# A block inverse on 128 partitions at once: 64x64 quadrant products replaced by 128x128 ones

## The chip, the core and the metric

The kernel runs on one core of a Trainium2 chip. A core has five engines that run side by side and meet only at semaphores: TensorE (PE, matrix products; its weight loads are shown as PEld), VectorE (DVE), ScalarE (ACT), GpSimd (POOL) and SyncE (SP, which here only starts DMAs). Each works through its own instructions in the order in which they were written. The metric is the device time of one launch in microseconds (us). The kernel before was timed three times: 1513.75, 1516.5 and 1520.16 us.

## The reference

Two transformer blocks in float32 on 256 tokens of width 1024. The first has differential and stick-breaking attention, cross attention and an MLP; the second has a latent attention (MLA), an RWKV-7 recurrence and a mixture of 16384 experts. The change touches the recurrence alone. The reference computes it token by token, per head, with a 64x64 state:

```
def rwkv7_step(state, inp):
    r_t, w_t, k_t, v_t, kk_t, a_t = inp
    sk = jnp.einsum('bhij,bhj->bhi', state, kk_t)
    state = (state * w_t[:, :, None, :]
             - sk[..., None] * (kk_t * a_t)[:, :, None, :]
             + v_t[..., None] * k_t[:, :, None, :])
    y = jnp.einsum('bhij,bhj->bhi', state, r_t)
    return state, y
```

The kernel takes 64 tokens at a time instead (a chunk; 4 chunks x 8 heads). Inside a chunk every token's update depends on those before it through a strictly triangular 64x64 matrix A, and the solution needs the inverse of I + A for each of the 32 pairs of chunk and head.

## The kernel before

All tensors lie with tokens or channels on the 128 partitions. Two chunks are stacked: partitions 0 to 63 hold the even chunk of a pair, 64 to 127 the odd one. So 32 inverses are 16 "problems" (`prob`), each with two chunks in it. Three tiles matter:

- `GB` (tile `hx`): per problem a 128x256 matrix; its first 128 columns are A transposed for both chunks, with zeros where the two chunks would mix (it was masked with `m2`).
- `Xc` and `Yc` (both in tile `pm`): per problem 64 columns, the inverse so far and its transpose, one chunk on each half of the partitions.
- `QX` (tile `pR`): an intermediate product, masked.

The inverse is built in levels. Level 0 is elementwise (`Yc` = I - masked A transposed; `Xc` = `Yc` transposed in 32x32 blocks on DVE). Each level l from 1 to 5 joins blocks of 2^l rows to blocks of twice that: a first product A·`Xc`, a mask (`lx{l}`, from the constants in tile `dst`), a second product with the inverse so far, a subtraction, and for l < 5 a transpose in 32x32 blocks. The 16 problems go in two groups of eight, j = 0 and 1, so that one group is on PE while the other is on DVE.

On PE, `quads` (L1049) makes one product for one group: 16 matrix products of 64x64 by 64x64, the even chunk's in the upper left quarter of the array, the odd chunk's in the lower right, each chunk into a PSUM bank of its own. The profile counts a float32 product as two records, so a call is 32 records of `64*64 64x64`. On DVE, each result is taken chunk by chunk, two operations of 64 partitions x 512 elements (L2283 for the mask, L2291 for the subtraction, both recorded at the helper's line L156), then one transpose (L177) that reads `Xc` and writes `Yc`. The first product of the next level waits for the subtraction; only its second product needs the transpose.

Other work is threaded between the levels, on every engine by the same written plan: the string list `PLAN` says, at each `turns.go()`, which parts take a step: "m" (MLA: squares, rotary embedding, `q2T` transposes, scores `m0` and `m1`, softmax), "t" (transposes of a, b, k, v to token order, `tok`), "k" (the products `GK`, masked into tile `prep`). Four `turns.go()` per level, on PE after each group's product, on DVE before each group's wait. So the order is fixed by hand, and whatever is late holds up what is written behind it.

PSUM has 8 banks. `bank` takes the one that was given back longest ago and waits until its reader is done; `give` names the reader.

`keep(n)` (L142) issues n products of the identity with itself into a bank that is free: 2n records `ps<-cst 128x128`, work without a use other than keeping PE from pausing. The table `KEEP` (L1057) puts 55 of them ahead of ten of the twenty `quads` calls, before the wait for that call's operand.

After level 5, ACT copies the even chunks of `Yc` to tile `rwY` (L1640) and DVE the odd ones (L2298); PE goes on with `values` (`vtok,prep`), which needs all of `GK`, and then with `solved_values` (`pR,rwY`).

Of the kernel before, what the change touches and what calls it, by code (L numbers as in the profile page):

```python
# [13 lines left out]
ALU = mybir.AluOpType  # L14
# [200 lines left out]
def bc(ap, axis, n):  # L215
    u = ap.unsqueeze(axis)
    shape = list(u.shape)
    shape[axis] = n
    return u.to_broadcast(shape)


def constants():
    p = np.arange(128)[:, None]
    f = np.arange(128)[None, :]
    one = lambda m: m.astype(np.float32)
    add = lambda m: np.where(m, 0.0, NEG).astype(np.float32)
    c = {"ident": one(p == f), "iota": np.broadcast_to(np.arange(128, dtype=np.float32), (128, 128)),
         "iota16": np.broadcast_to(np.arange(16, dtype=np.float32), (128, 16))}
    d = {}
    z = np.zeros((128, 128), np.float32)  # L230
    d["maskA"] = np.concatenate([z, add(f <= p)], 1)
    d["maskM"] = np.concatenate([z, add(f // 64 <= p // 64)], 1)
    d["maskS"] = one(p < f)
    d["negtri"] = -one(p >= f)
    d["negones"] = -np.ones((128, 128), np.float32)
    d["blk"] = one(p // 64 == f // 64)
    d["hsel"] = one(p // 64 == np.arange(2)[None, :])
    same = p // 64 == f // 64
    d["m2"] = np.concatenate([one(same & (p < f)), one(same & (p <= f))], 1)
    d["eye2"] = one(p % 64 == np.arange(64)[None, :])  # L240
    for l in range(6):
        m = 1 << l
        lev = (p // (2 * m) == f // (2 * m)) & (p // m % 2 == 1) & (f // m % 2 == 0)
        d[f"lx{l}"] = one(lev)[:, 0:64] + one(lev)[:, 64:128]
        d[f"ly{l}"] = one(lev.T)[:, 0:64] + one(lev.T)[:, 64:128]
    d["rst"] = np.broadcast_to(one(np.arange(256)[None, :] % 64 != 0), (128, 256))
    f1 = np.float32(500000.0) ** (-np.arange(0, 16, 2, dtype=np.float32) / np.float32(16))
    f2 = np.float32(10000.0) ** (-np.arange(16, dtype=np.float32) / np.float32(16))
    d["invf"] = np.broadcast_to(np.concatenate([f1, f2]).astype(np.float32), (128, 24))
    return c, d  # L250
# [10 lines left out]
def build(nc, T, poff, outs, stop=99):  # L261
# [4 lines left out]
    with ctx:  # L266
# [34 lines left out]
        def D(k): return dst[:, doff[k][0]:doff[k][1]]  # L301
# [31 lines left out]
        rt = P0[:, :, :].rearrange("p a b -> p (a b)").rearrange("p (i n d) -> p i n d", i=4, n=16)  # L333
# [82 lines left out]
        pRf = pR[:, :, :].rearrange("p a b -> p (a b)")  # L416
        f2 = lambda t: t[:, :, :].rearrange("p a b -> p (a b)")
        sg, x2_, y_ = hx[:, 0, 0, 0:256], ARt[:, :, 0, :], hx[:, 0, 1, :].rearrange("p (a b) -> p a b", b=256)
        GB = hx[:, :, :, :].rearrange("p i t n -> p (i t n)").rearrange("p (n d) -> p n d", d=256)
# [2 lines left out]
        ysq, TAT, nU = xm("ysq", [128, 16, 64]), xm("TAT", [128, 4, 256]), xm("nU", [128, 2, 512])  # L422
        pmf = pm[:, 0:8, :].rearrange("p a b -> p (a b)")
        c64 = lambda t, k: t[:, 1024 * k:1024 * k + 1024].rearrange("p (n d) -> p n d", d=64)
        QX, Xc, Yc = c64(pRf, 0), c64(pmf, 0), c64(pmf, 1)
        prob = lambda b_, r, i: (b_ * 2 + r) * 4 + i
        halves = [slice(64 * c, 64 * c + 64) for c in range(2)]
        parts = [(tb, lo, hi) for lo, hi in ((0, 384), (384, 640)) for tb in range(2)]
# [93 lines left out]
        def tensor(pe):  # L522
# [87 lines left out]
            for r in range(2):  # L610
                rs = slice(64 * r, 64 * r + 64)
                for hp in range(2):
                    b = pe.bank("z", (r, hp))
# [432 lines left out]

            turns = Turns(mla(), tokens(), products(1))

            def quads(key, lt, rt):  # L1049
                bs = [pe.bank("qd", (*key, c)) for c in range(2)]  # L1050
                for q in range(8):
                    for c, hs in enumerate(halves):
                        last = pe.mm(bs[c][hs, q * 64:q * 64 + 64], lt(c, hs, 8 * key[2] + q), rt(hs, 8 * key[2] + q), True, True)
                last.then_inc("qd_ps", key)


            KEEP = {(1, 0, 0): 3, (1, 1, 0): 4, (1, 1, 1): 5, (2, 0, 0): 15, (2, 0, 1): 9, (2, 1, 0): 3, (4, 1, 1): 3, (5, 0, 0): 5, (5, 1, 0): 5, (5, 1, 1): 3}  # L1057
            for l in range(1, 6):
                for j in range(2):
                    pe.keep(KEEP.get((l, 0, j), 0))  # L1060
                    pe.wait_ge("GB")
                    if l == 1:
                        pe.wait_ge("X0", j)
                    else:
                        pe.wait_ge("XY", (l - 1, j, 1))
                    quads((l, 0, j), lambda c, hs, p: GB[hs, p, 64 * c:64 * c + 64], lambda hs, p: Xc[hs, p, :])
                    turns.go()
                    for c in range(2):
                        pe.give("qd", (l, 0, j, c), "QX", (l, j, c))
                for j in range(2):  # L1070
                    pe.keep(KEEP.get((l, 1, j), 0))
                    pe.wait_ge("QX", (l, j, 1))
                    if l == 1:
                        pe.wait_ge("Y0", j)
                    else:
                        pe.wait_ge("Yt", (l - 1, j))
                    if l < 5:
                        quads((l, 1, j), lambda c, hs, p: Yc[hs, p, :], lambda hs, p: QX[hs, p, :])
                    else:
                        quads((l, 1, j), lambda c, hs, p: QX[hs, p, :], lambda hs, p: Yc[hs, p, :])  # L1080
                    turns.go()
                    for c in range(2):
                        pe.give("qd", (l, 1, j, c), "XY", (l, j, c))
            turns.end("t")
            turns.end("k")
            def values(b_):
# [239 lines left out]
        def scalar(act):  # L1326
# [308 lines left out]
                    turns.go()  # L1635
            turns.end("t")
            for j in range(2):
                act.wait_ge("XY", (5, j, 1))
            act.wait_ge("Y_z")
            act.act(Y[0:64, :, 0:64], Yc[0:64, :, :], ACT.Copy).then_inc("Y_a")  # L1640
            for _ in range(5):
# [107 lines left out]
        def vector(dve):  # L1749
# [522 lines left out]
                    yield  # L2272

            turns = Turns(mla(), tokens(), products(1))
            pv = lambda b, hs: b[hs, :].rearrange("p (a b) -> p a b", a=8)
            for l in range(1, 6):
                for j in range(2):
                    js = slice(8 * j, 8 * j + 8)
                    turns.go()
                    dve.wait_ge("qd_ps", (l, 0, j))  # L2280
                    dve.wait_ge("pm", 11)
                    for c, hs in enumerate(halves):
                        dve.tt(QX[hs, js, :], pv(dve.ps("qd", (l, 0, j, c)), hs), bc(D(f"lx{l}")[hs, :], 1, 8), ALU.mult).then_inc("QX", (l, j, c))  # L2283
                for j in range(2):
                    js = slice(8 * j, 8 * j + 8)
                    turns.go()
                    dve.wait_ge("qd_ps", (l, 1, j))
                    M = Xc if l < 5 else Yc
                    dve.wait_ge("X0" if l == 1 else "Yt", j if l == 1 else (l - 1, j))
                    for c, hs in enumerate(halves):  # L2290
                        v = dve.tt(M[hs, js, :], M[hs, js, :], pv(dve.ps("qd", (l, 1, j, c)), hs), ALU.subtract).then_inc("XY", (l, j, c))  # L2291
                    if l < 5:
                        dve.after(v)
                        dve.tr(Yc[:, js, :].rearrange("p a b -> p (a b)"), Xc[:, js, :].rearrange("p a b -> p (a b)")).then_inc("Yt", (l, j))
            turns.end("k")
            dve.wait_ge("XY")
            dve.wait_ge("Y_z")
# [528 lines left out]
```

## Times and profile before

| | |
|---|---|
| runs | 1513.75, 1516.5, 1520.16 us; median 1516.5 |
| profiled execution | 1519.88 us in all, of it a span of 1517.9 us from the first instruction to the last |
| PE busy | 1468.3 us, 97% of the span |
| DVE, ACT, POOL busy | 1035.8, 725.1, 239.1 us |
| the chain that ended last | PE 84%, DVE 10%, ACT 3% |
| the inverse, levels 1 to 5 with what is threaded between | 555.3 to 617.5 us of the span |

Starts are in us from the span's start. "x32" is the number of records merged into a row. A bracket at the end of a row is idle time of that engine ahead of it, and who ended it. Ends of matrix products are modelled and overlap the next ones, so the distance between the starts of two rows is the better measure of what a PE row takes.

### The profile page before, as it was taken

How to read it: one execution, taken by the hardware profiler on the slowest of the kernel's cores; microseconds unless marked ns; L12 is line 12 of the kernel's file. 1: busy time of each engine (PE TensorE's matmuls, PEld its weight loads, DVE VectorE, ACT ScalarE, POOL GpSimd, SP SyncE). 2: the span in 40 equal slices, each digit the busy share in tenths (PEclk: the TensorE clock that was granted, in tenths of full speed). 3: DMA queues.
4: the chain of work that ended last, by engine and by line, in shares of the span. 5: the costliest groups of instructions: out<-in, count | busy, mean ns of one | idle time of the engine just before them, and what ended most of it. 6: DMA issues, size and time to landing. Idle time of an engine off the chain costs nothing.

```text
span 1517.9 us, 25275 instructions
## 1 busy us (share of the span) xinstructions
PE 1468.3 (97%) x10480; PEld 1317.6 (87%) x10480; DVE 1035.8 (68%) x1832; ACT 725.1 (48%) x1195; POOL 239.1 (16%) x115
## 2 busy tenths in 40 slices
PE   7999999999998989999999999999999999999998
PEld 5897797998887878879999999999998888888886
DVE  5665455665449788663798799999955555555554
ACT  4564353554344634344544544444444444454453
POOL 0036000000014220538685000000000000000000
PEclk9999999999999989999999999999999999999999
DMA  7623442456662510044555544444455555656653
GB/s 275 214 97 126 141 150 97 157 181 195 190 178 73 174 57 2 21 128 155 175 188 187 178 154 142 152 143 150 143 178 171 189 189 187 192 185 189 192 185 123
DMA packets 64881, 235.28 MB, mean 155 GB/s; under 512 B 7424, under 2 KB 7680, under 8 KB 64512
## 3 DMA queue, kind: packets, MB, share of 16 engines
q1 hardware_dynamic: 63904, 231.60, 47.7%
q10 hardware_dynamic: 864, 2.08, 0.4%
q8 instruction: 83, 1.36, 0.4%
q14 instruction: 30, 0.25, 0.0%
HBM read 232.60 MB, written 1.05 MB: 154 GB/s over the span
## 4 chain that ended last, share of the span: by engine, by line
PE 84%; DVE 10%; ACT 3%; issue 1%; DMA 1%; POOL 0%; ACTq 0%; DVEq 0%; POOLq 0%
PE ps L131 83%; DVE spl L156 1%; PE ps L140 1%; ACT spl L153 1%; DVE pm L156 1%; DVE pR L156 1%; DVE prep L156 1%; DMA raw<-in_w_in_a 1%; DVE pm L165 1%; ACT QK L153 1%; DMA par<-in_par 1%; DVE zs L156 0%; DVE junk L156 0%; DVE hx L159 0%; ACT L153 0%
## 5 line engine op out<-in xcount | busy, mean ns | idle before, releaser
L131 PE MATMUL ps<-xhl,spl 128*128 128x256 f32 x4944 | 606.4, 283 | 3.4 <-POOL spl L156 1.6
L131 PEld LDWEIGHTS ps<-xhl,spl 128*128 128x128 f32 x4944 | 591.5, 189 | 6.2 <-issue 3.3
L156 DVE TENSOR_TENSOR spl<-raw,spl 128x1024 fp32r<-128x1024 f32 (+2 forms) x356 | 430.3, 1214 | 241.1 <-ACT spl L153 239.4
L153 ACT ACTIVATE spl<-raw 128x1024 fp32r<-128x1024 f32 (+1 forms) x435 | 454.4, 1048 | 284.8 <-PE ps L131 269.5
L131 PE MATMUL ps<-spl,Wr 128*128 128x512 f32 x1536 | 357.2, 395 | 1.1 <-DVE Wr L156 1.1
L131 PEld LDWEIGHTS ps<-spl,Wr 128*128 128x128 f32 x1536 | 289.3, 188 | 68.7 <-DVE Wr L156 1.3
L156 POOL TENSOR_TENSOR spl<-raw,spl 128x1024 fp32r<-128x1024 f32 x79 | 199.8, 2543 | 282.3 <-ACT spl L153 281.9
L153 ACT ACTIVATE Wr<-GE 128x256 fp32r<-128x256 f32 x128 | 53.3, 417 | 182.0 <-PE ps L131 182.0
L153 ACT ACTIVATE GE<-ps 128x256 f32<-128x256 f32 (+42 forms) x176 | 57.1, 327 | 126.5 <-DVE GE L156 109.8
L156 DVE TENSOR_TENSOR Wr<-GE,Wr 128x256 fp32r<-128x256 f32 x128 | 54.4, 425 | 79.8 <-ACT Wr L153 79.8
L131 PE MATMUL ps<-spl,ahl 128*128 128x512 f32 x384 | 90.1, 396 | 0.0
L131 PEld LDWEIGHTS ps<-spl,ahl 128*128 128x128 f32 x384 | 72.2, 188 | 17.6
L131 PE MATMUL ps<-spl,yhl 128*128 128x512 f32 x288 | 72.1, 410 | 3.3 <-DVE yhl L156 3.3
L131 PEld LDWEIGHTS ps<-spl,yhl 128*128 128x128 f32 x288 | 55.7, 195 | 16.9 <-issue 3.7
L156 DVE TENSOR_TENSOR Ao<-EB,gp 128x768 bf16<-128x768 bf16 x128 | 65.2, 551 | 0.0
L131 PE MATMUL ps<-spl,xhl 128*128 128x512 f32 (+2 forms) x288 | 62.1, 373 | 1.9 <-DVE spl L156 1.8
L131 PEld LDWEIGHTS ps<-spl,xhl 128*128 128x128 f32 x288 | 51.0, 188 | 12.1 <-DVE spl L156 3.4
L131 PE MATMUL ps<-Ao,EB 128*128 128x128 bf16 x768 | 55.8, 220 | 1.0 <-DVE Ao L156 1.0
L156 DVE TENSOR_TENSOR EB<-io,idx 128x512 bf16<-128x512 bf16 x128 | 48.2, 418 | 0.0
L131 PEld LDWEIGHTS ps<-Ao,EB 128*128 128x128 bf16 x768 | 44.7, 97 | 4.0 <-issue 1.2
L156 POOL TENSOR_TENSOR stats<-stats,neghalf 128x1 f32<-128x1 f32 (+2 forms) x13 | 8.0, 615 | 205.4 <-DVE stats L159 205.4
L153 ACT ACTIVATE gl<-ps 128x256 f32<-128x256 f32 (+32 forms) x81 | 24.1, 297 | 25.8 <-PE ps L131 25.8
(341 smaller groups left out, 1185.8 us busy)
## 6 DMA issues: line engine op xcount, KB each, us to landing
raw<-in_eu SPq DMA_DIRECT2D x128, 512.0 KB, 3.5
raw<-in_ev SPq DMA_DIRECT2D x128, 512.0 KB, 3.5
raw<-in_w_up SPq DMA_DIRECT2D x32, 512.0 KB, 3.6
raw<-in_w_down SPq DMA_DIRECT2D x32, 512.0 KB, 4.3
raw<-in_w_in_a SPq DMA_DIRECT2D x16, 512.0 KB, 5.2
raw<-in_w_pq SPq DMA_DIRECT2D x16, 512.0 KB, 3.5
raw<-in_w_rwkv SPq DMA_DIRECT2D x14, 512.0 KB, 3.8
raw<-in_w_in_t SPq DMA_DIRECT2D x8, 512.0 KB, 4.0
```

What stands on the lines that cost most here:

```text
L131: return Done(self, self.e and self.e.matmul(out, l, r, start=st, stop=sp))
L140: return Done(self, self.e and self.e.transpose(out, in_, self.ident[0:n, 0:n]))
L153: return Done(self, self.e and self.e.activation(out, a, f, bias=bias, scale=scale, accum_out=acc))
L156: return Done(self, self.e and self.e.tensor_tensor(out, a, b, op))
L165: return Done(self, self.e and self.e.scalar_tensor_tensor(out, a, s, b, o0, o1))
```

## The change

All sixteen problems' chunks are now treated as pairs on 128 partitions.

- PE: `octet` takes the place of `quads`: per problem one product with a 128x128 stationary matrix and 64 moving columns, 8 per call, into one PSUM bank instead of two. For the first product the stationary matrix is `GB[:, p, 0:128]`, for the second it is `QX[:, p, 0:128]`.
- `QX` is now 128 columns per problem: the mask `lx{l}` is 128 wide and zero where chunks would mix, and DVE reads the 64 columns of the bank twice (a broadcast axis), one operation of 128 x 1024.
- The second product is QX transposed times `Yc` at all levels, so DVE subtracts from `Yc` (one operation of 128 x 512), and the transpose writes `Xc`. The next level's first product therefore waits for the transpose (`Xt`) now.
- The table `KEEP` is gone; 9 identity products stay ahead of level 2's first product, behind its wait instead of before it.
- Constants: `lx1` to `lx5` are 128 columns wide, and `lx0` and `ly1` to `ly5`, which nothing read, are gone; `dst` goes from 2394 to 2330 columns.

```
-        QX, Xc, Yc = c64(pRf, 0), c64(pmf, 0), c64(pmf, 1)
+        QX, Xc, Yc = pRf[:, 0:2048].rearrange("p (n d) -> p n d", d=128), c64(pmf, 0), c64(pmf, 1)
...
-            def quads(key, lt, rt):
-                bs = [pe.bank("qd", (*key, c)) for c in range(2)]
+            def octet(key, lt, rt):
+                b = pe.bank("qd", key)
                 for q in range(8):
-                    for c, hs in enumerate(halves):
-                        last = pe.mm(bs[c][hs, q * 64:q * 64 + 64], lt(c, hs, 8 * key[2] + q), rt(hs, 8 * key[2] + q), True, True)
+                    p = 8 * key[2] + q
+                    last = pe.mm(b[:, q * 64:q * 64 + 64], lt[:, p, 0:128], rt[:, p, :], True, True)
                 last.then_inc("qd_ps", key)
-            KEEP = {(1, 0, 0): 3, (1, 1, 0): 4, (1, 1, 1): 5, (2, 0, 0): 15, (2, 0, 1): 9, (2, 1, 0): 3, (4, 1, 1): 3, (5, 0, 0): 5, (5, 1, 0): 5, (5, 1, 1): 3}
...
-                    pe.keep(KEEP.get((l, 0, j), 0))
                     if l == 1:
                         pe.wait_ge("X0", j)
                     else:
-                        pe.wait_ge("XY", (l - 1, j, 1))
-                    quads((l, 0, j), lambda c, hs, p: GB[hs, p, 64 * c:64 * c + 64], lambda hs, p: Xc[hs, p, :])
+                        pe.wait_ge("Xt", (l - 1, j))
+                    if (l, j) == (2, 0):
+                        pe.keep(9)
+                    octet((l, 0, j), GB, Xc)
                     turns.go()
...
-                    if l < 5:
-                        quads((l, 1, j), lambda c, hs, p: Yc[hs, p, :], lambda hs, p: QX[hs, p, :])
-                    else:
-                        quads((l, 1, j), lambda c, hs, p: QX[hs, p, :], lambda hs, p: Yc[hs, p, :])
+                    octet((l, 1, j), QX, Yc)
                     turns.go()
...
-                    for c, hs in enumerate(halves):
-                        dve.tt(QX[hs, js, :], pv(dve.ps("qd", (l, 0, j, c)), hs), bc(D(f"lx{l}")[hs, :], 1, 8), ALU.mult).then_inc("QX", (l, j, c))
+                    dve.tt(QX[:, js, :].rearrange("p n (c d) -> p n c d", c=2),
+                           bc(dve.ps("qd", (l, 0, j))[:, :].rearrange("p (n d) -> p n d", d=64), 2, 2),
+                           bc(D(f"lx{l}").rearrange("p (c d) -> p c d", c=2), 1, 8), ALU.mult).then_inc("QX", (l, j))
...
-                    M = Xc if l < 5 else Yc
-                    dve.wait_ge("X0" if l == 1 else "Yt", j if l == 1 else (l - 1, j))
-                    for c, hs in enumerate(halves):
-                        v = dve.tt(M[hs, js, :], M[hs, js, :], pv(dve.ps("qd", (l, 1, j, c)), hs), ALU.subtract).then_inc("XY", (l, j, c))
+                    v = dve.tt(Yc[:, js, :], Yc[:, js, :], dve.ps("qd", (l, 1, j))[:, :].rearrange("p (n d) -> p n d", d=64), ALU.subtract).then_inc("XY", (l, j))
                     if l < 5:
                         dve.after(v)
-                        dve.tr(Yc[:, js, :].rearrange("p a b -> p (a b)"), Xc[:, js, :].rearrange("p a b -> p (a b)")).then_inc("Yt", (l, j))
+                        dve.tr(Xc[:, js, :].rearrange("p a b -> p (a b)"), Yc[:, js, :].rearrange("p a b -> p (a b)")).then_inc("Xt", (l, j))
```

PE, end of level 1 and start of level 2, before (`pR,pm` is the second product of level 1, `cst,be` a token transpose, `cst` alone the identity products, `pm,hx` the first product of level 2):

```order
577 L131 MATMUL ps<-pR,pm 64x64 [waits Y0,QX]
578 L131 MATMUL ps<-pR,pm 64x64 x15
579 L140 MATMUL ps<-cst,be 128x128 [waits tok]
580 L140 MATMUL ps<-cst,be 128x128 x3
581 L131 MATMUL ps<-cst 128x128 x15
582 L131 MATMUL ps<-pm,hx 64x64 [waits XY]
583 L131 MATMUL ps<-pm,hx 64x64 x15
```

The same place in the changed kernel:

```order
572 L131 MATMUL ps<-pm,pR 128x64 [waits uq,Y0,QX]
573 L131 MATMUL ps<-pm,pR 128x64 x7
574 L140 MATMUL ps<-cst,be 128x128 [waits vM]
575 L140 MATMUL ps<-cst,be 128x128 x3
576 L131 MATMUL ps<-cst 128x128 [waits Xt]
577 L131 MATMUL ps<-cst 128x128 x8
578 L131 MATMUL ps<-pm,hx 128x64 [waits tok]
579 L131 MATMUL ps<-pm,hx 128x64 x7
```

Fifteen identity products stood ahead of the wait; nine stand behind it now, and the wait is for the transpose, `Xt`, not for the subtraction, `XY`.

DVE in level 1, before and after in one piece of the difference (`pR<-ps,dst` is the mask, `qst` and `mst` rows belong to MLA, `pm<-pm,ps` is the subtraction):

```order
 L165 SCALAR_TENSOR_TENSOR pm<-pm,par,pR 128x256 x3
-L156 TENSOR_TENSOR pR<-ps,dst 64x512 [waits pm,pe_ps]
-L156 TENSOR_TENSOR pR<-ps,dst 64x512
+L156 TENSOR_TENSOR pR<-ps,dst 128x1024 [waits pm,pe_ps]
 L171 TENSOR_REDUCE qst<-Mx 128x16 [waits act_sq]
 L159 TENSOR_SCALAR qst<-qst 128x16 [waits own_dve]
-L156 TENSOR_TENSOR pR<-ps,dst 64x512 [waits pe_ps]
-L156 TENSOR_TENSOR pR<-ps,dst 64x512
+L156 TENSOR_TENSOR pR<-ps,dst 128x1024 [waits pe_ps]
 L156 TENSOR_TENSOR junk<-QK,rows 128x256 [waits rope]
```

The neighbours keep their places; two operations become one. On ACT, POOL and SP no instruction is moved or changed but the load of `dst`, which is 64 columns narrower.

## Rows read from the trace of the kernel before

**Rows 1.** The page: busy time by engine, and the chain that ended last.
```profile
PE 1468.3 (97%) x10480; PEld 1317.6 (87%) x10480; DVE 1035.8 (68%) x1832; ACT 725.1 (48%) x1195; POOL 239.1 (16%) x115
PE 84%; DVE 10%; ACT 3%; issue 1%; DMA 1%; POOL 0%; ACTq 0%; DVEq 0%; POOLq 0%
```

**Rows 2.** Stretches: length, busy PE, PEld, DVE, ACT, POOL (records), PEclk, DMA, GB/s.
```profile
555.30:617.48 62.18, 57.58 (x897) 50.17 (x898) 56.89 (x89) 30.33 (x89) 11.85 (x8) 1.00 0.01 2
569.59:616.28 46.69, 43.31 (x688) 37.00 (x689) 41.96 (x65) 23.27 (x77) 4.22 (x4) 1.00 0.01 2
```

**Rows 3.** PE in order of time, levels 1 and 2: start, length, operation, idle before.
```profile
565.11 0.66 PE L140 MATMUL ps<-cst,be 128*128 128x128 f32 x4
565.60 3.51 PE L131 MATMUL ps<-cst 128*128 128x128 f32 x30
569.59 1.15 PE L131 MATMUL ps<-pm,hx 64*64 64x64 f32 x32 [0.48 <-DVE pm L156]
570.67 0.66 PE L140 MATMUL ps<-cst,ka 128*128 128x128 f32 x4
...
577.14 0.66 PE L140 MATMUL ps<-cst,ka 128*128 128x128 f32 x4
577.73 1.15 PE L131 MATMUL ps<-pR,pm 64*64 64x64 f32 x32
```

**Rows 4.** PE in order of time, behind the stage: full-array products of 64 columns.
```profile
616.28 1.97 PE L131 MATMUL ps<-vtok,prep 128*128 128x64 f32 x16 [0.80 <-DVE prep L156]
618.09 1.04 PE L140 MATMUL ps<-cst,Mx 128*128 128x128 f32 x8
618.97 1.90 PE L131 MATMUL ps<-vtok,prep 128*128 128x64 f32 x16
620.70 1.04 PE L140 MATMUL ps<-cst,Mx 128*128 128x128 f32 x8
```

**Rows 5.** DVE in order of time, level 1.
```profile
556.11 1.21 DVE L156 TENSOR_TENSOR pm<-pR 128x1024 f32<-128x1024 f32 x1
...
559.13 1.41 DVE L156 TENSOR_TENSOR pR<-ps,dst 64x512 f32<-64x512 f32 x2
560.57 1.75 DVE L171 TENSOR_REDUCE qst<-Mx 128x16 f32<-128x1536 f32 x1
...
568.13 1.40 DVE L156 TENSOR_TENSOR pm<-pm,ps 64x512 f32<-64x512 f32 x2
569.57 0.71 DVE L177 STREAM_TRANSPOSE pm<-pm 128x512 f32<-128x512 f32 x1
```

**Rows 6.** PE by kind, 569.5 to 616.2: the identity products. Busy us, mean ns, idle.
```profile
L131 PE MATMUL ps<-cst 128*128 128x128 f32 x56 | 7.7, 284 | 0.0
```

**Rows 7.** ACT in order of time, level 2.
```profile
571.86 8.59 ACT L153 ACTIVATE QK<-QK,qst 128x96 f32<-128x96 f32 x32
580.35 0.57 ACT L153 ACTIVATE ktok<-ps 128x512 f32<-128x512 f32 x1
```

**Rows 8.** DVE in order of time, levels 4 and 5: reductions between two masks.
```profile
599.02 1.22 DVE L171 TENSOR_REDUCE mst<-Mx 128x8 f32<-128x1024 f32 x1
...
605.29 2.28 DVE L171 TENSOR_REDUCE mst<-Mx 128x8 f32<-128x2048 f32 x1
```

**Rows 9.** PE in order of time: the first work after three pauses of PE.
```profile
167.39 24.27 PE L131 MATMUL ps<-spl,yhl 128*128 128x512 f32 x96 [3.32 <-DVE yhl L156]
...
486.15 3.64 PE L131 MATMUL ps<-be,dst 128*128 128x512 f32 x4 [1.68 <-DVE be L156]
...
534.58 2.37 PE L140 MATMUL ps<-cst,cn 128*128 128x128 f32 x10 [5.94 <-DVE cn L162]
```

**Rows 10.** Stretches at these pauses; columns as in rows 2.
```profile
169.00:170.00 1.00, 1.00 (x4) 0.81 (x3) 0.00 (x0) 0.00 (x0) 0.00 (x0) 0.50 0.00 0
486.00:490.00 4.00, 3.85 (x5) 1.30 (x6) 3.05 (x7) 0.00 (x0) 0.00 (x0) 0.57 0.00 0
531.00:541.00 10.00, 6.42 (x27) 5.11 (x28) 8.79 (x22) 2.59 (x8) 4.02 (x2) 0.50 0.33 105
```

More of the change, by code:

```diff
@@ L243, in constants @@
         lev = (p // (2 * m) == f // (2 * m)) & (p // m % 2 == 1) & (f // m % 2 == 0)
-        d[f"lx{l}"] = one(lev)[:, 0:64] + one(lev)[:, 64:128]
-        d[f"ly{l}"] = one(lev.T)[:, 0:64] + one(lev.T)[:, 64:128]
+        if l:
+            d[f"lx{l}"] = one(lev)
+        else:
+            d["ly0"] = one(lev.T)[:, 0:64] + one(lev.T)[:, 64:128]
     d["rst"] = np.broadcast_to(one(np.arange(256)[None, :] % 64 != 0), (128, 256))
@@ L1047, in tensor @@
             turns = Turns(mla(), tokens(), products(1))
-            def quads(key, lt, rt):
-                bs = [pe.bank("qd", (*key, c)) for c in range(2)]
+            def octet(key, lt, rt):
+                b = pe.bank("qd", key)
                 for q in range(8):
-                    for c, hs in enumerate(halves):
-                        last = pe.mm(bs[c][hs, q * 64:q * 64 + 64], lt(c, hs, 8 * key[2] + q), rt(hs, 8 * key[2] + q), True, True)
+                    p = 8 * key[2] + q
+                    last = pe.mm(b[:, q * 64:q * 64 + 64], lt[:, p, 0:128], rt[:, p, :], True, True)
                 last.then_inc("qd_ps", key)
-            KEEP = {(1, 0, 0): 3, (1, 1, 0): 4, (1, 1, 1): 5, (2, 0, 0): 15, (2, 0, 1): 9, (2, 1, 0): 3, (4, 1, 1): 3, (5, 0, 0): 5, (5, 1, 0): 5, (5, 1, 1): 3}
+            pe.wait_ge("GB")
             for l in range(1, 6):
                 for j in range(2):
-                    pe.keep(KEEP.get((l, 0, j), 0))
-                    pe.wait_ge("GB")
                     if l == 1:
@@ L1064, in tensor @@
                     else:
-                        pe.wait_ge("XY", (l - 1, j, 1))
-                    quads((l, 0, j), lambda c, hs, p: GB[hs, p, 64 * c:64 * c + 64], lambda hs, p: Xc[hs, p, :])
+                        pe.wait_ge("Xt", (l - 1, j))
+                    if (l, j) == (2, 0):
+                        pe.keep(9)
+                    octet((l, 0, j), GB, Xc)
                     turns.go()
-                    for c in range(2):
-                        pe.give("qd", (l, 0, j, c), "QX", (l, j, c))
+                    pe.give("qd", (l, 0, j), "QX", (l, j))
                 for j in range(2):
-                    pe.keep(KEEP.get((l, 1, j), 0))
-                    pe.wait_ge("QX", (l, j, 1))
+                    pe.wait_ge("QX", (l, j))
                     if l == 1:
                         pe.wait_ge("Y0", j)
-                    else:
-                        pe.wait_ge("Yt", (l - 1, j))
-                    if l < 5:
-                        quads((l, 1, j), lambda c, hs, p: Yc[hs, p, :], lambda hs, p: QX[hs, p, :])
-                    else:
-                        quads((l, 1, j), lambda c, hs, p: QX[hs, p, :], lambda hs, p: Yc[hs, p, :])
+                    octet((l, 1, j), QX, Yc)
                     turns.go()
-                    for c in range(2):
-                        pe.give("qd", (l, 1, j, c), "XY", (l, j, c))
+                    pe.give("qd", (l, 1, j), "XY", (l, j))
             turns.end("t")
@@ L1637, in scalar @@
             for j in range(2):
-                act.wait_ge("XY", (5, j, 1))
+                act.wait_ge("XY", (5, j))
             act.wait_ge("Y_z")
@@ L2274, in vector @@
             turns = Turns(mla(), tokens(), products(1))
-            pv = lambda b, hs: b[hs, :].rearrange("p (a b) -> p a b", a=8)
             for l in range(1, 6):
```

## The prediction, made before the changed kernel was run

> **What bounds the kernel now.** I began with the page. PE is busy 97% of the span and carries 84% of the chain that ended last [rows 1], so a change counts by what it does to the moment at which PE gets on with its next work. Then I read busy time by stretch. In the inverse (62.18 us, 4% of the span) two engines are nearly full: PE 57.58 and DVE 56.89; the granted clock is 1.00 and DMA is idle [rows 2]. Then both engines in order of time. There the chain runs back and forth: PE waits for a subtraction on DVE, DVE for a product. PE's own share is padded, since 55 identity products (KEEP's sum) fill waits. What follows the stage on PE (`vtok,prep`, from 616.28 [rows 4]) is full-array work, so I take a shift of that start as a shift of the kernel's end. The question is therefore when `vtok,prep` starts in the changed kernel.
>
> **PE: quads against octets.** A call of `quads` takes 1.08 us from its start to the next one's (569.59 to 570.67) [rows 3]. The octet has a twin in the trace: `vtok,prep`, eight float32 products, stationary 128x128, 64 moving columns. It takes 616.28 to 618.09 = 1.81 us after a wait and 618.97 to 620.70 = 1.73 without one [rows 4]. I take 1.75. Half as many products cost 0.67 us more per call, since a quarter-array product took 1.08/16 = 0.07 us and a full one takes 0.22. Over 20 calls that is +13.4 us of PE. Of the identity products 46 of 55 go; one takes 3.51/15 = 0.23 us [rows 3], so -10.8 us. Both are unhidden only where PE is not waiting anyway, so I walk through it.
>
> A rule of the Trainium skill speaks for the opposite price: TensorEngine Tiling, section Instruction Overhead, says that every matmul carries about 60 cycles of overhead and that one of very few columns takes as long as one of 60. Counted by that rule, half the matmuls are half the time, an octet of 0.54 us. The 0.22 us of rows 4 against 0.07 speaks against it here; the rival with the cheap octet stands below on its own rows.
>
> **DVE.** A mask was two operations, 1.44 us from 559.13 to 560.57 [rows 5]. Now it is one of 128x1024 that reads 512 PSUM columns twice. No row shows such a read. The nearest is the 128x1024 operation from SBUF, 1.21 us [rows 5]; lower end 0.70 (time by elements read: half the two-operation row of 1.41), upper end 1.44 (as two operations). I take 1.21, the row with the same output size. The subtraction goes from 1.44 (568.13 to 569.57) to 0.7. So DVE saves 10 x 0.23 + 10 x 0.72, about 9.5 us over the stage. The transpose, 0.71 us [rows 5], was beside the next first product and now stands before it.
>
> **Walk to level 2.** The first mask starts at 559.13 as before, because it waits for DVE's own work ahead of it. To the first subtraction DVE saves two masks, 0.5 us, and some 0.1 where operations overlap: it starts at 567.5 instead of 568.13. One operation, then the transpose: 567.5 + 0.7 + 0.04 + 0.71 = 568.95. PE has had nothing since its token transposes: the second product of group 1 starts when its mask is done, about 563.4, takes 1.8, and the transposes 0.5, so PE stands from 565.7 to about 568.95, 3.2 us. Before, 15 identity products covered that place, 565.60 to 569.1 [rows 3]. Now nine follow the wait, 2.1 us, and the octet starts at 571.0. Before it was 569.59: 1.4 us late. DVE has rotary work in the meantime, so it is held up only at the end.
>
> **Walk from level 2 to `vtok,prep`.** Before, 46.69 us from 569.59 to 616.28 [rows 2]. In it are 16 quads, 17.3 us; 28 identity products (56 records [rows 6]) of 0.23, 6.5 us; and pauses of 46.69 - 43.31 = 3.4 us [rows 2]. The remainder is 19.5. Two small things in it go with the quads: four transposes take 0.59 us ahead of quads (577.14 to 577.73) and 0.49 ahead of full-array work (565.11 to 565.60) [rows 3], some eight times, 0.8 us; and the end of a row lies 0.07 to 0.2 behind the next row's start, so each of about eight pauses is longer than shown, 1.2 us in all. That leaves 17.5 us of threaded work, which stays.
> After: 17.5 + 16 octets x 1.75 = 28.0, and the pauses that are left. I looked for them by following who feeds whom. (1) The token transpose of k must be evacuated by ACT, and behind it stand 32 scaled copies of 8.59 us, then the next evacuation of 0.57 [rows 7], which frees a bank. The copies start 2 us later than before, since ACT's first k evacuation sits behind the late octet; PE arrives about 0.2 us too early. (2) At level 5's first octet PE waits for mask, 1.22 us reduction [rows 8], subtraction, transpose: 1.2 + 1.2 + 0.7 + 0.7 + the last threaded product's evacuation 0.7, less overlap, 4.3 us against two octets of 3.5: 0.8. (3) At level 5 the mask stands behind the reduction of 2.28 us [rows 8]: another 0.8. Sum 1.8. All other waits are under the octets. So 17.5 + 28.0 + 1.8 = 47.3, and 571.0 + 47.3 = 618.3 against 616.28: +2.0 us. DVE's saved time ends as DVE idling: the stage has become PE's.
>
> **The clock.** PE pauses of 1.68, 3.32 and 5.94 us [rows 9] each come with a granted clock of 0.50, the lower level of 1.2 GHz, in the work behind them [rows 10]. At the pause of 1.68 us the mean of four us is 0.57, so 0.50 for 3.4 of them (0.43/0.50 x 4); at 5.94 us it is 0.50 for 10 us. The new pause of 3.2 us is like the one of 3.32. At half clock PE does half its work; some 3 us of it after 568.95 cost 1.5 us. I take 1.4. Lower end 0 (no fall), upper 5 (a fall of 10 us).
>
> Two things cost nothing: the narrower constants (a load far ahead of any wait) and the bank per call instead of two (no wait before is put down to a bank of the quads).
>
> **Sum.** +2.0 + 1.4 = +3.4 us. The working is in the time of the profiled execution, 1519.88 us with a span of 1517.9, which lies 3.4 above the median of 1516.5; the difference is applied to the median: 1519.9 us, 0.2% slower. A measurement of this kernel tells about 0.5%, 7.6 us, from no change, so I forecast no change that can be told.
>
> **The rivals.**
> A. *The forecast*: the octets' 0.67 us more, less the identity products, PE the bound from level 2 on, one clock fall. 1519.9, from 1517.5 (mask at 0.70 saves 0.2 us in each wait for DVE, no fall) to 1521.5 (mask at 1.44, each octet at 1.81). Chance 0.66.
> B. *Cheap octets (faster)*: if a full-array product with a new 64-column operand cost no more than a quarter-array one, 0.54 to 1.08 us per call, PE's part from level 2 shrinks by 16 x 0.67 = 10.7 us or more, but the chain through DVE then ends last, and only DVE's savings on it count: three or four levels of 1.0 to 1.9 us, 3 to 7 us. 1509.5 to 1513.5. The stationary operand is twice as wide in both directions, and rows 4 show the price of exactly this shape; what speaks for it is only that DVE was nearly as full as PE. Chance 0.08.
> C. *Nothing is left of it*: PE's waits absorb the longer calls, for instance because more of the 3.4 us of pauses and of the covered waits go than I counted, and the clock holds. 1515.5 to 1517.5. Chance 0.14.
> D. *The clock stays down (slower)*: after the pause at 565.7 the fall lasts as after 534.58, 10 us at 0.50, and levels 2 and 3, which are PE-bound by then, run at half speed: 5 us; and the waits for the masks in level 1 (0.5 and 0.9 us, formerly under identity products) bring a fall of 3.4 us of their own, 1.7 more. 1516.5 + 2.0 + 5 + 1.7 = 1525.2, slower by 0.6%. It decides once the low clock lasts beyond level 2. Against it: only the 5.94 us pause did that. Chance 0.12.
> That the change does not do what it says is excluded by the order of instructions.
>
> **Numbers.** Cases A and C lie within 0.5% whole (0.80). B stands just inside its edge (below 1508.9 is faster) and D just outside (above 1524.1 is slower); with the scatter of a measurement I give half of B, 0.04, to faster, and most of D, 0.10, with 0.01 from A, to slower: 0.11. Same 0.85. The runs of one kernel differ by 3 us either way of the median, so the range that should hold the time 8 times in 10 is 1513.5 to 1525.0.
>
> **What would show it.** Right: `pm,hx` and `pm,pR` rows of `128*128 128x64 x16` with 1.73 to 1.81 us from start to start; a PE pause of about 3 us ahead of nine identity products near 569, then PEclk 0.50 for a few us; the mask about 1.21 us; DVE busy some 9.5 us less in the stage and idle in between; `vtok,prep` at 618 to 620. Wrong: octets near 1.1 us, or `vtok,prep` before 616 (then DVE was the bound); PEclk 1.00 throughout (no third term); a mask over 1.5 us (then DVE has lost what it gained).

## The result, and the profile after

The changed kernel is slower: 1530.62 us median of 20 runs (from 1518.16 up) against 1517.99 for the kernel before (20 runs, 1513.75 to 1520.57); ratio 1.0064, 95% interval 1.0046 to 1.0081. One run of 6526.84 us is a disturbed one and enters no comparison.

The median hides two levels: 8 runs from 1518.16 to 1523.01 us and 11 from 1529.95 to 1536.14, nothing between. Each run also lists its granted clock as a mean, and since the clock is either 1.00 or 0.50, the time at 0.50 is span x (1 - clock) x 2. The lower level has 12 to 27 us of it, the upper 37 to 61; the 76 runs of the kernel before that list a clock have 9 to 30. A kernel whose end is set by PE should lose half of that time, so I also give each kernel's mean time less half of its time at 0.50, its "full-clock time": 1508.6 us before, 1509.1 after.

Half is too much, though. Within the 76 runs of the kernel before, one more us at 0.50 goes with 0.40 us more time (a straight line fitted to them), and within the 19 of the changed kernel it is 0.40 too. Carried to no time at 0.50 with that slope, the means are 1510.5 us before and 1512.8 after. So of the 9.2 us between the two means (1518.44 and 1527.65), about 7 are clock and 2.3 are there at full clock. Two kernels with much different time at 0.50 can be compared by the "full-clock time" only to some us (0.1 us for each us of that difference).

The profiled execution of the changed kernel took 1536.14 us (span 1534.3), the slowest of the upper level. From its page, then two stretches of it (length; busy PE, PEld, DVE, ACT, POOL; PEclk):

```profile
span 1534.3 us, 24419 instructions
PE 1483.2 (97%) x10068; PEld 1335.5 (87%) x10068; DVE 1027.5 (67%) x1812; ACT 725.4 (47%) x1195; POOL 238.8 (16%) x115
PE 86%; DVE 9%; ACT 2%; DMA 1%; issue 1%; POOL 0%; ACTq 0%; DVEq 0%; POOLq 0%
```
```profile
558.84:632.55 73.71, 68.63 (x475) 65.03 (x475) 47.18 (x69) 30.53 (x88) 10.09 (x6) 0.84 0.00 1
571.40:595.30 23.90, 23.25 (x111) 23.17 (x111) 9.22 (x15) 11.99 (x38) 2.74 (x2) 0.50 0.01 1
```

The stage, from PE's first octet to `vtok,prep`, takes 73.71 us. DVE's busy time in it is 47.18, against 56.89 in the 62.18 us of [rows 2]. For 23.90 us of it PE runs at half clock while it is busy for 23.25 of them. Not the whole difference to the profile before lies here: PE reaches the stage 3.4 us later (558.84 against 555.46), behind 30.6 us at 0.50 instead of 23.8 in work that the change does not touch, and the stage itself is 12.9 us longer (73.71 against 60.82). PE in order of time (start, length, operation, idle before), to set beside [rows 3] and [rows 4]:

```profile
558.84 1.97 PE L131 MATMUL ps<-pm,hx 128*128 128x64 f32 x16 [0.75 <-ACT QK L153]
...
568.54 0.61 PE L140 MATMUL ps<-cst,be 128*128 128x128 f32 x4
572.04 4.21 PE L131 MATMUL ps<-cst 128*128 128x128 f32 x18 [2.90 <-DVE pm L177]
576.05 3.51 PE L131 MATMUL ps<-pm,hx 128*128 128x64 f32 x16
...
594.50 2.28 PE L131 MATMUL ps<-pm,hx 128*128 128x64 f32 x16
...
602.71 1.90 PE L131 MATMUL ps<-pm,pR 128*128 128x64 f32 x16
604.44 2.00 PE L131 MATMUL ps<-qT 96*128 96x128 f32 x16
...
617.86 2.00 PE L131 MATMUL ps<-pm,hx 128*128 128x64 f32 x16 [0.47 <-DVE pm L177]
...
632.55 1.97 PE L131 MATMUL ps<-vtok,prep 128*128 128x64 f32 x16 [0.44 <-DVE prep L156]
```

The pause of 2.90 us at 569 is where it was expected. An octet takes 3.3 us behind it (576.05 to 579.36) and 1.73 once the clock is back (602.71 to 604.44). From 595.3 to the end of the stage the clock is 1.00, level 5 with its waits of 0.18 and 0.47 us included, although the octets are the same. DVE, beside [rows 5]: the mask that reads 512 PSUM columns twice, and the one-operation subtraction.

```profile
L156 DVE TENSOR_TENSOR pR<-ps,dst 128x1024 f32<-128x1024 f32 x10 | 12.2, 1220 | 12.6 <-PE ps L131 12.5
L156 DVE TENSOR_TENSOR pm<-pm,ps 128x512 f32<-128x512 f32 x10 | 6.8, 680 | 6.3 <-PE ps L131 6.3
```

Both cost what they were taken for (1.22 and 0.68 us), and the idle time at the row's end says what became of the saving: DVE waits for PE.

### The profile page after: what moved, and what is told of

It is laid out like the page before. It is cut to its first block, busy times and chain, and to the rows that moved or that the text cites. A ratio compares the mean times of both kernels' runs of the same rounds, so it can differ in the third digit from the quotient of the medians.

```text
span 1534.3 us, 24419 instructions
## 1 busy us (share of the span) xinstructions
PE 1483.2 (97%) x10068; PEld 1335.5 (87%) x10068; DVE 1027.5 (67%) x1812; ACT 725.4 (47%) x1195; POOL 238.8 (16%) x115
## 4 chain that ended last, share of the span: by engine, by line
PE 86%; DVE 9%; ACT 2%; DMA 1%; issue 1%; POOL 0%; ACTq 0%; DVEq 0%; POOLq 0%
PE ps L131 85%; PE ps L140 1%; DVE spl L156 1%; ACT spl L153 1%; DMA raw<-in_w_in_a 1%; DVE pm L165 1%; DMA par<-in_par 1%; DVE pR L156 0%; DVE pm L156 0%; DVE zs L156 0%; DVE junk L156 0%; DVE hx L159 0%; DVE prep L156 0%; ACT L153 0%; DVE xhl L165 0%
```

## The experiments

Theory O, as it stood after the result: the octets themselves keep the clock low. Its rival P: the pause at 569 does. All runs, each with the comparison to the kernel before as it was run in the same job:

| kernel | runs | median us | ratio, 95% interval | mean us at 0.50 | full-clock time |
|---|---|---|---|---|---|
| before (in the three jobs of e1 to e12) | 76 | 1518.5 | | 20 | 1508.6 |
| the changed kernel | 19 | 1530.0 | 1.0064, 1.0046 to 1.0081 | 37 | 1509.1 |
| e1_keep_ahead | 6 | 1526.7 | 1.0051, 1.0032 to 1.0069 | 36 | 1508.9 |
| e2_no_keep | 5 | 1535.8 | 1.0111, 1.0090 to 1.0133 | 56 | 1507.7 |
| e3_before_pause | 12 | 1523.3 | 1.0024, 1.0008 to 1.0039 | 32 | 1506.0 |
| e4_keep24_behind | 12 | 1524.9 | 1.0080, 1.0046 to 1.0113 | 36 | 1512.4 |
| e5_wide | 5 | 1523.3 | 1.0041, 1.0028 to 1.0054 | 27 | 1510.4 |
| e6_wide_ahead | 11 | 1519.2 | 1.0013, 1.0002 to 1.0024 | 23 | 1508.7 |
| e7_split_subtract | 12 | 1519.9 | 1.0018, 1.0005 to 1.0031 | 19 | 1511.2 |
| e8_wide_no_keep | 11 | 1520.3 | 1.0010, 1.0000 to 1.0020 | 25 | 1508.1 |
| e9_filler_64 | 12 | 1518.4 | 0.9993, 0.9981 to 1.0006 | 16 | 1510.1 |
| e10_wide_to_3 | 7 | 1528.1 | 1.0058, 1.0037 to 1.0078 | 38 | 1508.2 |
| e11_wide_from_4 | 12 | 1519.5 | 1.0017, 0.9999 to 1.0034 | 22 | 1509.7 |
| e12_full_filler | 6 | 1525.5 | 1.0041, 1.0025 to 1.0057 | 24 | 1512.8 |

All ratios lie within 2% of 1, so the differences are read from their intervals. Each row has one profile; of the other runs only the sum at 0.50 is known, and that sum does not say where it lies. The profile of e8_wide_no_keep, for one, has 43 us of it, and only 6.8 in the stage. The listed clock has three decimals, so the time at 0.50 of one run is known to about 1.5 us.

### Is it the pause?

**e1_keep_ahead** fills the pause:

```
+                    if (l, j) == (2, 0):
+                        pe.keep(15)
                     if l == 1:
                         pe.wait_ge("X0", j)
                     else:
                         pe.wait_ge("Xt", (l - 1, j))
-                    if (l, j) == (2, 0):
-                        pe.keep(9)
```

> The changed kernel with 15 identity products ahead of the wait for the transpose (level 2, group 0) and none behind it, so that PE's pause of 2.9 us at 569 is filled. Theory P (the pause starts the low clock): the granted clock stays 1.00 from there on, the runs of 1530 to 1536 us vanish, and the 9 products less behind the wait give back up to 2.1 us: 1516 to 1519 us in every run. Theory O (the octets themselves keep the clock down, pause or not): runs at 1528 to 1534 us remain, about half of them.

Neither came out as written. The upper level of 1530 to 1536 is gone, but so is the lower one: 1524.65 to 1529.82 us. Two stretches of it, columns as above, and PE where the clock fell:

```profile
566.30:600.70 34.40, 32.92 (x280) 32.00 (x279) 22.90 (x33) 16.00 (x47) 1.83 (x2) 1.00 0.00 1
600.70:624.60 23.90, 23.90 (x97) 19.81 (x97) 10.71 (x14) 6.56 (x30) 2.38 (x2) 0.50 0.00 1
```
```profile
552.82 1.97 PE L131 MATMUL ps<-pm,hx 128*128 128x64 f32 x16 [0.75 <-ACT QK L153]
...
597.54 2.00 PE L131 MATMUL ps<-pm,pR 128*128 128x64 f32 x16 [0.18 <-DVE pR L156]
600.00 3.03 PE L131 MATMUL ps<-pm,hx 128*128 128x64 f32 x16 [0.47 <-DVE pm L177]
602.96 2.07 PE L131 MATMUL ps<-ARt,ka 64*128 64x256 f32 x4
...
625.04 1.97 PE L131 MATMUL ps<-vtok,prep 128*128 128x64 f32 x16
```

With the pause filled the clock stays at 1.00 through levels 2 to 4, with the octets of 64 columns there. Then it falls at 600.7, behind waits of 0.18 and 0.47 us only, and stays at 0.50 for 23.90 us in which PE is busy without a gap. So a pause like the one at 569 is not needed, and octets alone do not always bring the fall: their surroundings or their place count too. All six runs have 30 us or more at 0.50.

**e2_no_keep** has no identity product at all (the two lines with `keep(9)` are taken out).

> The changed kernel without any identity product. Theory P: the pause is as long as before or longer, so the low clock comes in as many runs or more; without the 9 products behind the wait a run without the fall is 1 to 2 us faster (1516 to 1521), one with it 1526 to 1534. If the low clock lasts because of what PE does behind the pause (octets and transposes), it lasts at least as long as the 23.9 us seen. Theory O: the same two levels of time as the changed kernel.

Slower than theory P's range in four of five runs (1532.15 to 1538.72), and theory O's lower level is not there either. Its profile has both stretches, the one behind the pause and the one at level 5:

```profile
563.00:580.00 17.00, 17.00 (x83) 16.96 (x83) 8.24 (x13) 10.64 (x36) 1.77 (x2) 0.50 0.00 0
604.00:634.70 30.70, 30.70 (x130) 26.61 (x129) 14.00 (x18) 9.90 (x36) 8.55 (x4) 0.50 0.00 1
```

It has 56 us at 0.50 in the mean against 37 with the nine products behind the wait. Those cost 9 x 0.23 = 2.1 us at full clock at most and are worth more than that by what they do to the clock.

**e3_before_pause** takes `(2, 0, 0): 15` out of the kernel before's table.

> The kernel before (quarter-array products) without the 15 identity products ahead of level 2, so that it has a pause of about 3.5 us there. If the pause alone starts the low clock, runs some us slower appear here too; if how long it lasts hangs on the octets, it is one stretch of 3.4 us and costs 1 to 2 us (1517 to 1521 us); if it hangs on the stage whatever the products are, 20 us or more at 0.50 and 1524 to 1532 us in some runs.

Two levels here too: five runs of 1517.35 to 1519.44 us, with 15 to 30 us at 0.50, and seven of 1523.18 to 1527.39 with 37 to 46. The profile shows one of the first level, with one short fall behind the pause:

```profile
565.30:568.70 3.40, 2.96 (x37) 2.85 (x38) 3.30 (x9) 0.00 (x0) 2.02 (x2) 0.51 0.02 5
568.70:612.00 43.30, 40.63 (x646) 34.74 (x645) 37.39 (x55) 22.66 (x76) 1.00 (x2) 1.00 0.01 2
```

So an uncovered pause at this place is dear with quads as well; where the seven longer runs are at 0.50 no profile shows. If it is in the stage, a long fall behind a pause needs no octets, and the experiments do not exclude that. The low full-clock time of 1506.0 does not mean that PE gets on faster without the 15 products: in the profile the stage takes 62.14 us (551.59 to 613.73) with 3.4 at 0.50, against 60.82 before, so at full clock the same within half a us.

**e4_keep24_behind** puts 24 in place of 9 behind the wait.

> The changed kernel with 24 identity products of 128 columns behind the wait instead of 9. They cost 15 x 0.23 = 3.4 us at full clock. If dense 128-column products bring the clock back where octets do not, the long stretches at 0.50 end within them: all runs lie close together, 1522 to 1527 us. If the length of the low clock does not hang on what PE runs, both levels of time stay and both rise by 3.4 us: 1523 and 1536.

Inconclusive for its purpose: seven runs of 1521.06 to 1525.46 us (12 to 24 us at 0.50), five of 1538.71 to 1541.79 (55 to 62). The two levels stay; by their means the lower rises by 3.0 us, as reckoned, and the upper by 7.0. The profile is of the lower level, with 3.4 us at 0.50 behind the pause; where the five longer runs have theirs is not shown. All that can be said is that a block of identity products behind the pause does not remove the upper level. The full-clock time rises by 3.3 us (15 x 0.23 = 3.4 expected).

### Is it the octets' few columns?

A float32 product of an octet shows in the profile as two weight loads with a stream of 64 columns behind each (16 records for 8 products). **e5_wide** streams 128 and changes nothing else; each product's surplus lands where the next one writes its own result:

```
-                    last = pe.mm(b[:, q * 64:q * 64 + 64], lt[:, p, 0:128], rt[:, p, :], True, True)
+                    if q < 7:
+                        last = pe.mm(b[:, q * 64:q * 64 + 128].rearrange("p (a b) -> p a b", a=2), lt[:, p, 0:128], rt[:, p:p + 2, :], True, True)
+                    else:
+                        last = pe.mm(b[:, q * 64:q * 64 + 64], lt[:, p, 0:128], rt[:, p, :], True, True)
```

> The changed kernel, but each product of an octet except the eighth streams 128 columns, its own 64 and the next problem's 64 (the next product overwrites those with the right ones). Loads, order and results stay the same; an octet should stay at 1.75 to 1.85 us, as identity products of 128 columns take 0.23 us each. Theory O2 (the low clock is kept on by products that stream few columns for each weight load): the stretch behind the pause at 569 is 3.4 to 7 us, never 24; all runs 1517 to 1523. Theory P2 (the pause sets it, and its length does not hang on the products): both levels of time stay, 1518 to 1523 and 1530 to 1536.

As theory O2 said (few columns behind each load keep the clock low): no run of the upper level; 21 to 34 us at 0.50 in five runs, and in the profile one fall of 3.4 us behind the pause. Its time is at the top of the range given and over it (1522.62 to 1526.66, three of five above 1523). The stage, and the fall:

```profile
554.19:619.08 64.89, 59.36 (x474) 55.70 (x475) 47.16 (x69) 29.98 (x88) 10.09 (x6) 0.97 0.01 1
567.90:571.30 3.40, 3.40 (x18) 3.40 (x18) 2.81 (x7) 0.00 (x0) 1.59 (x2) 0.51 0.00 0
```

**e6_wide_ahead** is the same edit on top of e1_keep_ahead.

> As e5_wide, with 15 identity products ahead of the wait for the transpose and none behind it. Theory O2: no low clock in the whole stage, neither at level 2 nor at level 5 where e1_keep_ahead had 23.9 us of it: 1514 to 1520 us in every run, so at or under the kernel before. Theory P2: since e1_keep_ahead had its low clock without the pause, another cause at level 5 stays, 1524 to 1530.

No low clock in the whole stage of the profile, at either place: 1518.2 to 1523.88 us, ratio 1.0013; four of eleven runs lie over the 1520 expected, with 27 to 33 us at 0.50 instead of 18. Against e1_keep_ahead, whose instructions differ by the streamed columns alone, 7.5 us of the median are back, and the stage takes 61.86 us instead of 72.22 (552.82 to 625.04). So 23.90 us at 0.50 cost 10.4 us, 0.43 of their length and not half: some waits vanish when PE is slow (0.26 and 0.44 us in level 5 and behind it). The two kernels ran in different jobs on different chips; e10_wide_to_3 below brings the low stretch back on the chip of this one. The stage, and PE where e1_keep_ahead ran the same octets:

```profile
553.36:615.22 61.86, 58.87 (x487) 55.34 (x487) 47.06 (x69) 29.95 (x88) 10.08 (x6) 1.00 0.01 1
```
```profile
563.50 3.51 PE L131 MATMUL ps<-cst 128*128 128x128 f32 x30
566.85 1.90 PE L131 MATMUL ps<-pm,hx 128*128 128x128 f32 x16
568.59 0.61 PE L140 MATMUL ps<-cst,ka 128*128 128x128 f32 x4
```

An octet of 128 columns takes 566.85 to 568.59, 1.74 us, as one of 64 does (1.73). The extra columns are free, so it is not they that set the price; the weight loads are what is left of it. The Trainium skill (TensorE: Matmul & The Clock Gate, section LDWEIGHTS) gives a load its number of columns divided by 1.2, in ns, whatever the rows. By that, 16 loads of 128 columns are an estimated 1.71 us, and the traces at a clock of 1.00 agree (1.73 and 1.74); at 0.50 they do not, the octet took 3.3 us there.

**e8_wide_no_keep** is e5_wide without an identity product.

> e5_wide without any identity product, so with the uncovered pause of 2.9 us at 569. Theory O2: one fall of 3.4 to 7 us and no more, 1516 to 1521 us, where e2_no_keep, the same with 64 columns, had 48 us at 0.50 and a median of 1535.8. Theory P2: as e2_no_keep, 1530 or more.

1517.01 to 1526.25 us, median 1520.3, where the same kernel with 64 columns had 1535.8; four of eleven runs lie over the 1521 expected. The profile is of the slowest, and most of its time at 0.50 lies outside the stage. Its pause of 2.90 us is uncovered, and the fall behind it lasts 6.8 us; levels 3 to 5 keep the clock:

```profile
571.30:578.10 6.80, 6.16 (x29) 6.16 (x30) 5.19 (x10) 1.60 (x6) 2.74 (x2) 0.50 0.00 1
578.10:622.00 43.90, 42.84 (x349) 39.99 (x347) 29.41 (x38) 21.52 (x73) 1.67 (x1) 1.00 0.01 1
```

**e10_wide_to_3** and **e11_wide_from_4** put the wide products at part of the levels of e1_keep_ahead (`if q < 7 and key[0] <= 3` and `key[0] >= 4`).

> e1_keep_ahead with 128 columns streamed at levels 1 to 3 and 64 at levels 4 and 5. Theory O2: the low stretch that e1_keep_ahead had from 600.7 on is set by the narrow octets of levels 4 and 5, so it comes back: 23 us or so at 0.50 there, 1524 to 1530 us in most runs.

> e1_keep_ahead with 64 columns at levels 1 to 3 and 128 at levels 4 and 5. Theory O2: no low stretch at levels 4 and 5, and none at level 2 because of the filler: 1514 to 1522 us as e6_wide_ahead. If instead the pause-free e1_keep_ahead fell for another reason at level 5 (its waits of 0.2 to 0.5 us), this one falls too: 1524 to 1530.

As theory O2 said. With narrow octets at levels 4 and 5 the low stretch returns at the same place as in e1_keep_ahead (1524.84 to 1530.25 us in six of seven runs, 1520.53 in one); with wide ones there it does not (nine of twelve runs up to 1520.93; three of 1525.58 to 1527.28 with 34 to 37 us at 0.50, which no profile shows). First a stretch of e10_wide_to_3, then one of e11_wide_from_4:

```profile
599.10:623.00 23.90, 23.90 (x97) 19.81 (x97) 10.46 (x14) 6.76 (x31) 1.95 (x2) 0.50 0.00 1
```
```profile
600.00:615.00 15.00, 14.00 (x104) 11.86 (x105) 11.94 (x18) 7.82 (x33) 1.90 (x1) 1.00 0.01 2
```

PE is fully busy in the one at 0.50 and has pauses in the one at 1.00. So being busy is not enough to hold the clock. Nor do narrow octets lower it everywhere: at levels 1 to 3 of e11_wide_from_4 they ran at 1.00. Over all profiles, with narrow octets at level 5 the clock fell there in three of six (e1_keep_ahead, e2_no_keep, e10_wide_to_3) and not in the changed kernel, e4_keep24_behind and e12_full_filler; with wide ones it fell in none of six.

**e9_filler_64** is e6_wide_ahead with 64 columns in the 15 identity products (`self.ident[:, 0:m]`, m = 64).

> e6_wide_ahead, but the 15 identity products that fill the pause at 569 stream 64 columns instead of 128; by the octets' rows they take the same 0.23 us each. If columns decide (theory O2), this filler works less well: with the narrow octets just ahead gone it may still hold, so either 1517 to 1523 as e6_wide_ahead or, if the clock falls at level 2, one stretch of 3.4 to 7 us more and 1 to 3 us more time. If only PE being busy decides, no difference to e6_wide_ahead at all.

No fall at level 2 in the profile; 1514.66 to 1522.29 us, ratio 0.9993 with 1 inside the interval. Between octets of 128 columns the filler's own width made no difference, so this run does not tell more than that.

**e12_full_filler** puts the whole `KEEP` table of the kernel before ahead of the waits of e1_keep_ahead.

> e1_keep_ahead (narrow octets) with the whole table of 55 identity products of the kernel before, each ahead of its wait. In the kernel before they stood in waits; now most of the 28 behind level 2's start do not, 0.23 us each, so 4 to 6 us more at full clock than e1_keep_ahead. Theory O2: they stream 128 columns and shorten or remove the low stretch (23.9 us, 12 us of time): 1513 to 1524. If padding cannot make up for narrow octets: 1528 to 1536.

1522.39 to 1526.51 us, between the two ranges given for most runs. The low stretch of the stage is gone from the profile. The price is 5.1 us in the stage over e6_wide_ahead, which has no low clock either (552.99 to 619.96, 66.97 us, against 61.86), as reckoned: half of what the low stretch cost, and PE has no idle left (66.57 of 67.00 us busy). And the clock falls behind the stage instead, for 10.2 us from 652.3 on, where e1_keep_ahead and e6_wide_ahead have 1.00. So padding saves only 1.2 us of e1_keep_ahead's median:

```profile
552.99 0.94 PE L131 MATMUL ps<-cst 128*128 128x128 f32 x6 [0.66 <-ACT QK L153]
...
619.96 1.97 PE L131 MATMUL ps<-vtok,prep 128*128 128x64 f32 x16 [0.43 <-DVE prep L156]
```
```profile
553.00:620.00 67.00, 66.57 (x567) 64.09 (x567) 47.31 (x69) 30.27 (x88) 10.18 (x7) 1.00 0.00 1
```

### What is DVE's saving worth?

**e7_split_subtract** makes the subtraction two operations of 64 partitions again, in e6_wide_ahead:

```
-                    v = dve.tt(Yc[:, js, :], Yc[:, js, :], dve.ps("qd", (l, 1, j))[:, :].rearrange("p (n d) -> p n d", d=64), ALU.subtract).then_inc("XY", (l, j))
+                    for hs in halves:
+                        v = dve.tt(Yc[hs, js, :], Yc[hs, js, :], dve.ps("qd", (l, 1, j))[hs, :].rearrange("p (n d) -> p n d", d=64), ALU.subtract)
+                    v = v.then_inc("XY", (l, j))
```

> e6_wide_ahead with DVE's subtraction as two operations of 64 partitions again, 10 x 0.72 us more on DVE. If PE is the bound of the stage from level 2 on, as the prediction says, only level 1 and the waits at levels 4 and 5 see it: 1 to 3 us more than e6_wide_ahead. If DVE still is: 5 to 7 us more.

Full-clock time +2.4 us, within the 1 to 3 expected, and in the profiles the stage takes 64.03 against 61.86, +2.2, for 6.4 us more of DVE busy time (53.48 against 47.06). PE is the bound of most of the stage; DVE sets it in level 1 and in two waits.

```profile
551.50:615.53 64.03, 59.10 (x486) 55.38 (x487) 53.48 (x78) 30.05 (x88) 10.06 (x6) 1.00 0.01 1
```

## Why the prediction was wrong

The measured 1530.62 us lies 5.6 above the range. Its working fails at one step, **the clock**: "I take 1.4. Lower end 0 (no fall), upper 5 (a fall of 10 us)". In the profiled execution the fall lasted 23.9 us and cost about 10 us (0.43 of its length, by e1_keep_ahead against e6_wide_ahead), and the 11 runs of the upper level have 30 us more at 0.50 than the 8 of the lower and take 12.7 us longer. I read how long a fall lasts from falls behind pauses elsewhere [rows 9, 10], as if the pause set it. Behind those pauses stood other work. Even the longest was misread: the low clock at 531 to 541 had begun at 530.7, inside the pause that ended at 534.58, so only 6.4 us of it lay in work. What the runs showed in its place is that the products bear on it: with 64 streamed columns for each weight load, the clock in some stretches fell and stayed down for 17 to 31 us while PE was busy nearly or wholly throughout (changed kernel, e1_keep_ahead, e2_no_keep, e10_wide_to_3); with 128, at the same places and the same length of octet, it fell for 3.4 to 6.8 us behind the pause and not at all without one (e5_wide, e6_wide_ahead, e8_wide_no_keep). What decides between the two levels from run to run of one kernel stays open. The forecast's other term, +2.0 us at full clock, was about right.

Point by point:

- *Octet 1.75 us.* Right: 1.73. The identity products at 0.23 us: right.
- *Mask 1.21, subtraction 0.7, DVE 9.5 us less.* Right on the two rows, 1.22 and 0.68. For the whole, 56.89 of rows 2 is over a stretch a little longer; from PE's first product of the stage to `vtok,prep` it is 55.60 before and 47.18 after, 8.4 us less.
- *Pause of 3.2 us ahead of level 2.* Right: 2.90.
- *The wait for ACT's scaled copies, 0.2 us.* None in the profile of the changed kernel, where PE was slow at that place; 0.47 us in e5_wide, where it was not. The other two waits of 0.8 each were 0.65 (0.18 + 0.47) and 0.26; another, 0.44 for the last `GK` mask, was taken as nothing. Sum 1.35, or 1.8 with the 0.47, against 1.8: right, with its parts wrong.
- *`vtok,prep` 2.0 us later at full clock.* About right. In the kernel before PE's first product of the stage is the row below, and 616.28 - 555.46 = 60.82. e5_wide, whose order, number and length of PE operations are the changed kernel's, takes 64.89, less half of 3.4 us at 0.50: 63.2, so +2.4. The changed kernel's own 73.71, less 0.43 x 23.9, gives 63.4. Whole runs give +2.3, as worked out in the section on the result.

```profile
555.46 0.94 PE L131 MATMUL ps<-cst 128*128 128x128 f32 x6 [0.66 <-ACT QK L153]
```

- *Rival D, 0.12.* It described the profiled run, and by their times probably the 11 of the upper level: a low clock that lasts beyond level 2. Its size (5 us, with 1.7 for a second fall) and its reason were wrong. It said that a pause as long as this would decide; e1_keep_ahead has no such pause and falls all the same.
- *Rival B (cheap octets).* Refuted by the price. *Rival C:* e6_wide_ahead is nearly that case, with the octets' columns doubled: +1.0 us in the stage (61.86 against 60.82).
- *The rule of the Trainium skill* (TensorEngine Tiling (Array Packing), section Instruction Overhead) was rightly not followed: by it an octet would take 0.54 us, and it took 1.73.

The largest fault lies in the reasoning on `KEEP`. I counted its 55 products as padding to be removed from PE's work and priced the one pause that they had covered. What e3_before_pause shows is that they bear on the clock: without 15 of them the kernel before, too, has about 20 us more at 0.50 in seven of twelve runs than in the other five. The prediction never asked what the new mix of products would do to the clock where PE does not pause.

Open: why the changed kernel, in its profile and, by their times, in its runs of the lower level, escapes the fall at level 5 that e1_keep_ahead's profile has, though the two are alike from there on; where the longer runs of e3_before_pause, e4_keep24_behind and e11_wide_from_4 are at 0.50; and what tells a run of one level from one of the other. No version beats the kernel before: e9_filler_64, the best of those with octets, is equal to it within 0.2%.

## What to carry to other kernels

Before replacing small products in quarters of the array by full-array ones, compare what rows of each shape take and do not count matmuls: 16 quarter-array products took 1.08 us, 8 full ones 1.73. Then look at PE's clock after the change, run by run, and not only at its busy time: a PE that spends its time on weight loads with few columns behind each can be fully busy at half clock. Here, streaming more columns (the neighbour's, overwritten by the next product) cost nothing and gave back 7 us of the median. And filler products that look like waste may be holding the clock: without 15 of them the kernel before lost 4.6 us of its median (e3_before_pause).

## What was not expected of the hardware

- The clock fell without a long pause: at 600.7 in e1_keep_ahead, behind waits of 0.18 and 0.47 us.
- It did not come back under steady work: 23.90 us at 0.50 with PE busy for all 23.90 of them in e1_keep_ahead, 30.70 of 30.70 in e2_no_keep. Between octets, PE did token transposes or `ARt,ka` products in these stretches.
- A float32 product of a 128x128 stationary matrix costs the same with 64 and with 128 streamed columns (octets of 1.73 and 1.74 us).
- The kernel before is itself spread by the clock: its 76 runs from 1513.98 to 1523.5 us have 9 to 30 us at 0.50, and 0.40 of the difference in the one is the difference in the other.
